# Operands of a scan and a short convolution loaded in swapped blocks and turned by VectorE, with four waits moved

## The reference

```python
def first_block(x, ...):
    proj = rmsnorm(x, g_mix) @ w_in
    y_sb = stick_breaking_attention(q_sb, k_sb, v_sb)      # 8 heads
    y_ca = chunked_relpos_attention(q_ca, k_ca, v_ca, rel_bias)
    merged = sigmoid(gate_sb) * (y_sb @ w_sb_out) + sigmoid(gate_ca) * (y_ca @ w_ca_out)
    x = x + merged @ w_mix_out
    x = x + (silu(g_ff) * u_ff) @ w_ffn_out
    x = x + sigmoid(rmsnorm(x, g_ple) @ w_ple_gate) * (p @ w_ple_in)
    return rmsnorm(x, g_final)

def even_layer(x, mem_n, ...):
    sc_b, sc_c, sc_v, sc_z, ssd_z, ssd_xbc, ssd_dt, mq, mz = split(rms_norm(x) @ w_in)
    y_a = sc_b * causal_depthwise_conv(sc_c * sc_v, sc_conv_w) * silu(sc_z)   # 3 taps, width 1024
    xbc = silu(causal_depthwise_conv(ssd_xbc, ssd_conv_w) + ssd_conv_b)        # 4 taps, width 3072
    y_b = ssd_chunked(xs, dt, a, bm, cm)   # a scan over chunks of 128, 32 heads in 4 groups
    ...
    return x + concatenate([y_a, y_b, y_m]) @ w_out

def odd_layer(x, mem_n, ...):      # latent attention: 16 heads, causal, with rope
    ...
```

## Time and profile before

| | us |
|---|---|
| median of 3 runs | 2681.97 |
| lowest, highest | 2680.12, 2685.82 |
| the profiled execution | 2681.47 |
| its span in the trace | 2679.9 |
| PE busy in it | 2651.9 (99%) |
| DVE, ACT busy | 1552.4 (58%), 1349.4 (50%) |

### The profile page before, as it was taken

The page is one execution under the profiler, slowest core; times in us unless marked ns, Lnnn a source line. Parts: engine busy times, 40 slices in busy tenths (PEclk is TensorE's granted clock), DMA queues, the critical chain, the costliest instruction groups (busy, mean ns, idle before and its releaser), DMA issues.

```text
span 2679.9 us, 35985 instructions
## 1 busy us (share of the span) xinstructions
PE 2651.9 (99%) x12119; PEld 2202.8 (82%) x12119; DVE 1552.4 (58%) x1824; ACT 1349.4 (50%) x1787; POOL 330.5 (12%) x507
## 2 busy tenths in 40 slices
PE   9999999999999999999999999999999999999998
PEld 7888888887888888888888878888888889888887
DVE  6444456656555555555454664446777755457764
ACT  6544455654444444444444554446565445554443
POOL 2100032211100000000000111001110100123300
PEclk9999999999999999999999999999999999999999
DMA  8966676677876767677676876666667776686565
GB/s 304 315 220 218 216 232 222 204 252 231 255 224 212 224 207 219 214 224 225 216 220 212 260 226 225 209 205 238 222 225 227 242 244 216 224 269 209 174 215 163
DMA packets 170482, 606.97 MB, mean 226 GB/s; under 512 B 22688, under 2 KB 22736, under 8 KB 169616
## 3 DMA queue, kind: packets, MB, share of 16 engines
q1 hardware_dynamic: 133632, 485.03, 55.4%
q0 software_dynamic: 36032, 119.50, 14.6%
q10 hardware_dynamic: 720, 1.11, 0.1%
HBM read 556.22 MB, written 50.90 MB: 227 GB/s over the span
## 4 chain that ended last, share of the span: by engine, by line
PE 89%; DMA 3%; DVE 3%; issue 3%; ACT 1%; POOL 1%; POOLq 0%; ACTq 0%; SPq 0%; DVEq 0%
PE acc L795 56%; PE acc L801 28%; DMA r_b<-d_x 1%; DMA d_x<-tile 1%; DMA d_h<-tile 1%; DVE w_lo L1819 1%; PE turn L1084 1%; ACT w_hi L1278 1%; POOL r_b L551 0%; PE ps_s L1221 0%; PE ps_s L1222 0%; DMA h_b<-d_h 0%; PE ps_y L886 0%; PE ps_y L989 0%; PE ps_s L873 0%
## 5 line engine op out<-in xcount | busy, mean ns | idle before, releaser
L1819 DVE TENSOR_TENSOR w_lo<-raw,w_hi 128x1024 fp32r<-128x1024 f32 x919 | 1117.5, 1223 | 880.2 <-ACT w_hi L1278 874.0
L1278 ACT ACTIVATE w_hi<-raw 128x1024 fp32r<-128x1024 f32 x919 | 964.8, 1060 | 894.3 <-PE acc L801 807.4
L795 PE MATMUL acc<-w_hi,x_t_hi 128*128 128x512 f32 (+1 forms) x2400 | 950.3, 396 | 4.6 <-ACT w_hi L1278 4.6
L795 PE MATMUL acc<-w_hi,x_t_lo 128*128 128x512 f32 (+1 forms) x2400 | 933.0, 389 | 0.0
L801 PE MATMUL acc<-w_lo,x_t_hi 128*128 128x512 f32 (+1 forms) x2400 | 640.0, 388 | 0.0
L795 PEld LDWEIGHTS acc<-w_hi,x_t_hi 128*128 128x128 f32 x2400 | 450.9, 188 | 96.9 <-ACT w_hi L1278 6.1
L801 PEld LDWEIGHTS acc<-w_lo,x_t_hi 128*128 128x128 f32 x2400 | 450.4, 188 | 92.5 <-DVE w_lo L1819 0.3
L795 PEld LDWEIGHTS acc<-w_hi,x_t_lo 128*128 128x128 f32 x2400 | 450.9, 188 | 90.5 <-issue 1.9
L795 PE MATMUL acc<-w_hi,ff_t_hi 128*128 128x512 f32 x352 | 136.9, 389 | 0.0
L795 PE MATMUL acc<-w_hi,ff_t_lo 128*128 128x512 f32 x352 | 136.9, 389 | 0.0
L801 PE MATMUL acc<-w_lo,ff_t_hi 128*128 128x512 f32 x352 | 94.1, 389 | 0.0
(11 more groups left out here) (400 smaller groups left out, 2696.1 us busy)
## 6 DMA issues: line engine op xcount, KB each, us to landing
raw<-stream SPq DMA_DIRECT2D x919, 512.0 KB, 4.3
d_in<-tile POOLq DMA_DIRECT2D x20, 512.0 KB, 3.7
d_ev<-tile POOLq DMA_DIRECT2D x20, 512.0 KB, 4.5
d_x<-tile POOLq DMA_DIRECT2D x16, 512.0 KB, 4.7
xin<-d_x POOLq DMA_DIRECT2D x16, 512.0 KB, 7.2
d_h<-tile POOLq DMA_DIRECT2D x14, 512.0 KB, 6.4
h_b<-d_h POOLq DMA_DIRECT2D x56, 128.0 KB, 4.5
r_b<-d_x POOLq DMA_DIRECT2D x52, 128.0 KB, 5.7
```

The costliest lines, as they stand in the source:

```text
L795: nc.tensor.matmul(out, src[x][:, chunk + c, t * P:(t + 1) * P], w_hi[:, s, w], start=first and c == 0 and x == 0, stop=False)
L1278: nc.scalar.activation(w_hi[:, u.slot, :], raw[:, u.slot, :], ACT.Copy).then_inc(hi_ready, 1)
L1819: nc.vector.tensor_tensor(w_lo[:, s, :], raw[:, s, :], w_hi[:, s, :].bitcast(F32), ALU.subtract).then_inc(lo_ready, 1)
```

## The change

Six edits, in one kernel:

- **Scan.** The host orders the weights' columns so that each 768-column group of the projection comes out in blocks of 32 by quarter. POOL reads it with four DMAs of 32 partitions into `u_b` (a quarter of the partitions each, 8 x 192), and DVE turns all 32x32 blocks with one instruction, `turn_u`, at place 15 of the stage or group before, into `u_t` in SBUF. PE's 12 transposes of each group are gone, ACT and DVE read `u_t`.
- **Short convolution.** The same: `sc_in` arrives by four DMAs of 32 partitions, DVE turns both operands with a 128x1024 instruction each (`sc_u`, `sc_w`) at place 7j+8, the taps read SBUF, and `sc_y` is one instruction. PE's 16 transposes of each half are gone.
- **Attention.** `HEAD_AT_UNIT` goes from (1, 3, 6, 9) to (1, 3, 5, 9): head J2 comes a unit earlier on PE, ACT and DVE.
- **Stage `out`.** On POOL the gates are loaded behind a block's store and read-back.
- **Stage `gate`.** On ACT the square of `x_raw` stands a place later (`raw_out`), and for the last block just ahead of the square of `tile`.
- **Latent heads.** `turn_pair` stands at place 4j-1, behind `rotate`, where it stood at 4j.

```diff
-HEAD_AT_UNIT = (1, 3, 6, 9)
+HEAD_AT_UNIT = (1, 3, 5, 9)
...
+    u_b = place("u_b", [P, TOK // SQ, 6 * SQ], F32, AT + 8 * K)
+    u_t = place("u_t", [P, 6, TOK], F32, END + 8 * K)
...
-    sc_in, sc_cv, sc_y = row_of(AT, ("sc_in", [P, TH, 4, NBW], F32), ("sc_cv", [P, 4, TOK], F32),
-                                ("sc_y", [P, 4 * TOK], F32))
+    sc_in, sc_cv, sc_y, sc_u, sc_w = row_of(
+        AT, ("sc_in", [P, TOK // SQ, 4, P], F32), ("sc_cv", [P, 4, TOK], F32), ("sc_y", [P, 4 * TOK], F32),
+        ("sc_u", [P, 4, TOK], F32), ("sc_w", [P, 4, TOK], F32))
...
         for n in range(BY_DVE["out"]):
-            if n < 2:
-                load_gates(n, (n + 2) * NBW, n + 3)
             pool.wait_ge(tile_ready, n + 3)
             pool.dma_start(halves(d_h), tile[0][:, :, :]).then_inc(blocks_in, 16)
             pool.wait_ge(blocks_in, OUT_MOVES * n + 16)
             load_blocks(h_b, d_h, TURN["mix"] + n)
+            if n < 2:
+                load_gates(n, (n + 2) * NBW, n + 3)
...
         def load_u(g):
-            pool.dma_start(u_in[:, :, 0:512], ev_v[:, :, bass.ds(g.times(512, 1024), 512)]).then_inc(s_u, 16)
-            for m in range(2):
-                pool.dma_start(u_in[:, :, 512 + m * P:640 + m * P],
-                               ev_v[:, :, bass.ds(g.times(P, 3072 + 512 * m), P)]).then_inc(s_u, 16)
+            for b in range(P // SQ):
+                w = 1024 + 768 * g.k + 6 * SQ * b
+                pool.dma_start(u_b[b * SQ:(b + 1) * SQ, :, :],
+                               d_ev[:, w:w + 6 * SQ].rearrange("(a j) n -> j a n", j=SQ)).then_inc(s_u, 16)
...
         def load_short(j):
-            for t in range(TH):
-                pool.dma_start(sc_in[:, t, :, :].rearrange("p a n -> p (a n)"),
-                               ev_v[:, t, 6144 + 2048 * j:6144 + 2048 * (j + 1)]).then_inc(c_in, 16)
+            for b in range(P // SQ):
+                w = 6144 + 2048 * j + NBW * b
+                pool.dma_start(sc_in[b * SQ:(b + 1) * SQ, :, :, :].rearrange("p a k n -> p a (k n)"),
+                               d_ev[:, w:w + NBW].rearrange("(a j) n -> j a n", j=SQ)).then_inc(c_in, 16)
...
-        pool.wait_ge(c_ut, 2)
-        pool.wait_ge(c_wt, 2)
+        pool.wait_ge(c_ut, 1)
+        pool.wait_ge(c_wt, 1)
...
-            if p == 0:
-                pe.wait_ge(s_u, n.times(48, 48))
+            if p == 7:
                 pe.wait_ge(dt_v, 7)
                 pe.wait_ge(s_yb, n.times(1, 1))
-                for c in range(6):
-                    bank = (turn[0], turn[1], ps_s)[c // 2]
-                    for t in range(TH):
-                        mm = nc.tensor.transpose(bank[:, (c % 2 * TH + t) * P:(c % 2 * TH + t + 1) * P],
-                                                 u_in[:, t, c * P:(c + 1) * P], ident[:, :])
-                mm.then_inc(s_ut, 1)
-            if p == 7:
                 pe.wait_ge(s_silu, n.times(1, 1))
...
-        def short(p, j):
-            if p == 8 + 7 * j:
-
-                if j:
-                    pe.wait_ge(c_y, j)
-                else:
-                    pe.wait_ge(turn_lo, 2 * TURN["x4"] + 2)
-                pe.wait_ge(c_u, j + 1)
-                pe.wait_ge(c_w, j + 1)
-                for src, banks, s_ in ((sc_in[:, :, 1, :], turn, c_ut), (sc_in[:, :, 0, :], (ps_s, ps_y), c_wt)):
-                    for h in range(2):
-                        for c in range(2):
-                            for t in range(TH):
-                                mm = nc.tensor.transpose(
-                                    banks[h][:, (c * TH + t) * P:(c * TH + t + 1) * P],
-                                    src[:, t, (2 * h + c) * P:(2 * h + c + 1) * P], ident[:, :])
-                        mm.then_inc(s_, 1)
-
...
+            def raw_out(b):
+                if gate:
+                    act.wait_ge(pl_sum, b + 1)
+                    square(x_raw, 32, At(b), count + 2 * b)
+
             def tile_out(b):
                 act.wait_ge(*ready(b))
                 square(tile[b % 2], col, At(b), count + b if gate is None else count + 2 * b + 1)
 
             def last_out():
...
+                    if b and k == 1:
+                        raw_out(b - 1)
...
-            act.wait_ge(pl_sum, b + 1)
-            square(x_raw, 32, At(b), 16 + 2 * b)
...
-                    bank = (turn[0], turn[1], ps_s)[c // 2]
                     ch = At(c + 4 * g) if c < 4 else At(12 + 4 * (c - 3) + g)
-                    last = nc.scalar.activation(cv[:, c, :], bank[:, c % 2 * TOK:(c % 2 + 1) * TOK], ACT.Identity,
+                    last = nc.scalar.activation(cv[:, c, :], u_t[:, c, :], ACT.Identity,
...
+        def turn_u(g):
+
+            dve.wait_ge(s_u, 64 * (g + 1))
+            dve.wait_ge(s_conv, 3 * g)
+            nc.vector.transpose(u_t[:, :, :].rearrange("p c (a i) -> p c a i", i=SQ),
+                                u_b[:, :, :].rearrange("p a (c i) -> p c a i", i=SQ)).then_inc(s_ut, 1)
+
+        def ez_beside(p):
+            time_steps(p)
+            if p == 15:
+                turn_u(0)
+
+        splits("ez", 16, 0, 0, 0, ez_beside)
...
-                    bank = (turn[0], turn[1], ps_s)[c // 2]
-                    u = bank[:, c % 2 * TOK:(c % 2 + 1) * TOK - back]
+                    u = u_t[:, c, 0:TOK - back]
...
+            if p == 15 and g < 3:
+                turn_u(g + 1)
...
-                dve.wait_ge(c_ut, 2 * j + 2)
+                for src, dst, ready, done in ((1, sc_u, c_u, c_ut), (0, sc_w, c_w, c_wt)):
+                    dve.wait_ge(ready, j + 1)
+                    dve.wait_ge(c_y, j)
+                    nc.vector.transpose(dst[:, :, :].rearrange("p c (a i) -> p c a i", i=SQ),
+                                        sc_in[:, :, src, :].rearrange("p a (c i) -> p c a i", i=SQ)).then_inc(done, 1)
+                dve.wait_ge(c_ut, j + 1)
                 for tap in (2, 1, 0):
                     back = 2 - tap
                     if back:
                         dve.wait_ge(c_conv, 3 * j + back)
                     for c in range(4):
-                        u = turn[c // 2][:, c % 2 * TOK:c % 2 * TOK + TOK - back]
...
-                dve.wait_ge(c_wt, 2 * j + 2)
+                dve.wait_ge(c_wt, j + 1)
                 dve.wait_ge(c_conv, 3 * j + 3)
-                for h in range(2):
-                    last = nc.vector.tensor_tensor(
-                        sc_y[:, 2 * h * TOK:2 * (h + 1) * TOK], (ps_s, ps_y)[h][:, :],
-                        sc_cv[:, 2 * h:2 * h + 2, :].rearrange("p c t -> p (c t)"), ALU.mult)
-                last.then_inc(c_y, 1)
+                nc.vector.tensor_tensor(sc_y[:, :], sc_w[:, :, :].rearrange("p c t -> p (c t)"),
+                                        sc_cv[:, :, :].rearrange("p c t -> p (c t)"), ALU.mult).then_inc(c_y, 1)
...
-            if p % 4 == 0 and 0 < p < 32:
-                turn_pair(p // 4)
...
                 rotate((p + 1) // 4)
+                turn_pair((p + 1) // 4)
...
-    ein = np.concatenate([w0[:, 9248:EVW], w0[:, 6144:9216], w0[:, 4096:6144]], axis=1)
+    xbc = np.concatenate([w0[:, 6144:8192].reshape(D, 4, 4, 4, SQ)] + [
+        w0[:, at:at + 512].reshape(D, 4, 1, 4, SQ) for at in (8192, 8704)], axis=2).transpose(0, 1, 3, 2, 4)
+    ein = np.concatenate([w0[:, 9248:EVW], xbc.reshape(D, -1), w0[:, 4096:6144]], axis=1)
...
-    short = np.concatenate([w0[:, 1024 * m + NBW * j:1024 * m + NBW * (j + 1)]
-                            for j in range(2) for m in range(4)], axis=1)
+    short = w0[:, :4096].reshape(D, 4, 2, 4, 4, SQ).transpose(0, 2, 4, 1, 3, 5).reshape(D, -1)
```

7 lines of the change are left out of this document (3 added, 4 removed).

## The result

| | before | after |
|---|---|---|
| median of 7 runs, us | 2681.28 | 2692.99 |
| lowest, highest | 2678.92, 2685.82 | 2689.98, 2699.11 |
| the profiled execution, its span | 2681.47, 2679.9 | 2699.11, 2697.6 |
| PE busy | 2651.9 | 2655.6 |
| mean granted clock of the profiled execution | 0.998 | 0.994 |

The ratio is 1.0043 (95% interval 1.0034 to 1.0053): 11.7 us slower, where I had forecast 6.5 us faster and nothing beyond 2684. The profiled execution of after is the slowest of its seven, 6 us above their median, so its stages are read for where, and the ratios of the runs for how much.

The account below looks back on a forecast made before the run. PE was taken as the bound, busy 2651.9 of 2679.9 us. Scan 0, short convolution -2.0, attention +6.4, out -4.6, gate -1.4, latent -4.9 sum to -6.5: 2681.47 to 2675.0 us, range 2664 to 2684.

Parts of the forecast that it names:

- Rival D: Stage out and latent heads: moved waits gain nothing because the next thing is as late; -9.5 goes, 2684.5 us; chance 0.07.
- the 2.53 of the sum: Attention, L886: PE's stall for J1's copy into `p_t` grows from 0.92 to 2.53 us, four times, +6.4 us.
- rival C: Attention and stage gate: PE's granted clock falls behind longer idle times, 5 x 1.7 = 8.5 us, 2683.5; chance 0.19, full or part.
- Rival A: Attention: the four waits of 0.92 us vanish, -3.7 in place of +6.4, total 2664.9 us; chance 0.17.
- So the chain does not move when the transposes go: Scan: DVE's chain from taps to states stays put, so PE's 1.36 us a group returns as waits; net 0.
- rival B: Scan: PE alone decides, so 5.4 us come through, and the short convolution's 1.6 too; 2668.0 us; chance 0.10.
- hidden in the idle time of DVE before the first taps: Scan: DVE's turn, some 1.9 us for 1536 columns, costs nothing; without that cover up to 1.9 us a group.
- POOL's two loads become four, behind the same wait: Short convolution: the loads split on POOL, with no cost counted in the term of -2.0 us.
- the 1.6 of the sum: Short convolution, second half: PE waits 1.6 us for `w_lo`, the middle of 0.6 and 2.4, against 3.6 saved.
- This loop goes round by DMA, not by PE: Stage gate: store and reload set the block loop, so earlier `w_hi` waits become `tile` waits; only the last gains, -1.4.
- The bound of +0.3: Stage gate: worse end of the -1.4 us term, with PE idle up to 2.7 us before L832 and a clock fall, +1.7.
- Its loads are old by then: Latent heads: `turn_pair`, some 4 us earlier, finds its loads landed; three `lqk` waits of 1.64 us go, -4.9.

## Why the prediction was wrong

**The path was right, the sum was not.** The term for stage out was right, those for scan, gate, latent and short convolution were each too good by 2.4 to 6.7 us, and so was the attention's, by 5.7. Rival D, that the moved waits gain nothing, fell. The step common to most of it is the clock: the sum took 1.7 us for the fall that goes in stage out and nothing for the falls that come. There are seven. At some 1.5 us each (an estimate, from the steps of the attention) they are about 10 of the 24.2 us by which the profiled execution missed the sum (17.67 against -6.5). The rest is waiting that I priced too low or at nothing.

**Attention (+6.4; measured +12.07, alone +11.23): the waiting was right, the clock was left out.** Order and durations held to 0.01 us, and in three of four iterations so did the stall: 2.52 us alone, 2.52 to 2.54 in after, for the 2.53 of the sum. In the first iteration `z_sb` came 0.4 us (alone) and 0.9 us (in after) later relative to PE than the whole unit that I counted, and the sum with the measured lead gives that stall too: 4.71 + 0.61 - 1.51 - 0.91 = 2.90 us alone, 3.38 in after. Why `z_sb` is later there I did not take apart. That makes 7.3 us of waiting in after. Of the rest, 4.5 are three falls of the clock at 1.5 us, a term that stood in the sum at nothing and in rival C at 1.7 for each of four. So rival C was right in its mechanism, in the attention and at the end of stage gate. Rival A fell as a forecast of this change, though its 3.7 us were real: the two kernels with the moved copy gained 4.1 and 4.3.

**Scan (0; measured +2.39, alone +2.97).** "So the chain does not move when the transposes go" held: of the 5.4 us that left PE none came through, and rival B fell. The step that failed is "hidden in the idle time of DVE before the first taps". In the first group ACT waits 0.9 us for the turn, which place 13 mended. The waits foreseen at L1065 and L1076, 1.5 us a group, are 1.7 us in all (L1061 and L1072 of after). What is left, +1.77, sits in them and in waits for `w_lo` and `z_t_lo` that I had not counted; that the earlier PE reaches DVE's full stretch with less lead fits it, and no run here separates it further.

**Short convolution (-2.0; measured +4.72, alone +3.65).** Two steps failed. "POOL's two loads become four, behind the same wait" was wrong twice. The wait is now for DVE's `sc_w` turn, not for PE's transposes, which by itself moved the issue by no more than 0.2 us within the stage. And four DMAs of 32 partitions land in up to 11.3 us alone and 11.9 in after, not 7.4. And I counted one stretch of DVE against PE's first L801 behind it, when the whole burst, with weights arriving late, pushed a `w_lo` to a wait of 4.57 us for the 1.6 of the sum, with a fall of the clock behind it. Spreading the burst took off 4.7 us with the split load still there, which shows the burst as the larger part; the split load alone costs 2.42 us with no turns on DVE, so the two overlap. The Trainium skill's "VectorE: DVE Perf Modes", section "Rules for kernel authors", which keeps such transposes on TensorE, had the sign of both parts as they stood, though part of that cost is the load's and not the engine's; with the burst spread, the runs with and without the turned short convolution (0.9938 and 0.9937) neither bear it out nor speak against it.

**Stage out (-4.6; measured -4.63): right,** the wait and the clock behind it. That it agrees to 0.03 us is luck in part, since the stage moves by -1.2 to +2.0 us where it is unchanged. The window of 1586 to 1590 above, and the earlier trace rows, show what such a wait costs; after the change stage out has neither.

**Stage gate (-1.4; measured +3.27, alone +2.97).** "This loop goes round by DMA, not by PE" was the failed step. It does go by DMA, but its time depends on when the units' `w_hi` and `w_lo` are made. `r_b` was issued at 1565.11 and DVE could turn it at 1576.13, 11.0 us later, with a wait of 5.05 in it. The loop became 1.1 us a block longer. That it is longer with the square moved in all blocks, and in no other kernel, the runs show. How, stays open. My reading is that an earlier `w_hi` lets several `w_lo` run at once, so that their slots come free together and the weight loads meet the block's store and reload. That is not shown: `r_b` itself took as long from issue to landing as before (median 7.5 us in both). POOL's waits for the store rose from 6.8 to 9.2 us in the three blocks, but 8.5 to 8.8 stand in six kernels that leave these blocks alone, too. Behind PE's waits of 1.91 and 2.45 us the clock fell. The bound of +0.3 was too near.

**Latent (-4.9; measured -1.21).** "Its loads are old by then" holds for pairs 2 and on and is wrong for pair 1: `k_b` is issued at 2457.11, and DVE stands 4.62 us for it. The three waits of before went, as forecast, and a new one of 1.80 us came, with the clock at 0.80 and 0.78 behind it: 3.7 us together (-1.21 against -4.9). The term's size was right for the other pairs, as -4.18 to -4.89 show where pair 1 stays.

**The spread.** My range ended at 2684 because I let only the clock push upward, and only in the attention and stage gate. The ends of the terms other than the attention's reached +1.0 and +0.3 at most, so that four errors of the same sign, each 2 to 7 us, were outside what I had allowed for. Three of my figures don't add up either: the sum's own range by its ends is 2670 to 2678, not 2672; the attention's upper bound is 6.4 + 4 x 1.7 = 13.2, not 13.4; and the chances named for "faster" add to 0.65, not 0.62.

## What to carry over

An in-order engine turns a moved step into a moved queue: before moving one, list what stands behind its first wait on that engine, and move the single late instruction (here a copy of 0.55 us, worth 15.5 us in its stage) rather than the whole block. Giving PE's work to an engine that is 58% busy costs when it lands as one burst among the operand halves that PE waits for; spread it over several places before judging it. A forecast wait as long as one behind which the clock fell wants that fall in the sum, not only in a rival: here stalls of 2.52 us brought it three times in four iterations. And a load that a change splits, or lets start at another time, has a new landing time that belongs in the sum with a wide end.

## What the runs showed of the hardware

- The same 2 MB took up to 7.4 us to land as two DMAs of 128 partitions, and up to 11.3 us as four of 32.
- Issued 16 us earlier within the stage, it took up to 16.0 us, and ACT stood 5.23 us for a weight unit around then. What else was in flight there I did not take apart.
- With a wait in the same place each iteration, the granted clock stayed at 1.00 behind the first, of 3.22 us idle in after and 2.74 in the attention alone, and fell behind the next three, of 2.37 each, to 0.57 and 0.77 over the 4 us that follow the second. It also fell behind 1.91 us in stage gate (0.59) and 1.80 in the latent heads (0.78 to 0.80), where before it stayed at 1.00 around one of 1.8. Idle length alone does not tell them apart here. Behind waits of 4.57 and 2.45 us the windows show 0.59 and 0.61.
- Such a fall cost 1.5 us in the attention, beside the wait itself.
- DVE turned 128x1024 float32 in 1.20 to 1.25 us and 128x1536 in 1.77. Its first tap of 128x256 took 0.35 us from SBUF, where it took 0.48 from PSUM; the taps of two operands and a factor took 0.48 from either (all medians of their groups).
